# Chunked attention with the values as weights and a feature-major result, one pipeline step deeper

## What is computed

```python
scores = jnp.einsum("bcqhd,bckhd->bhcqk", qc, kb).astype(jnp.float32) * (dh ** -0.5)
scores = scores + rel_bias_band(rel_bias).astype(jnp.float32)[None, :, None]
...
probs = jax.nn.softmax(scores, axis=-1).astype(v.dtype)
out = jnp.einsum("bhcqk,bckhd->bcqhd", probs, vb)
...
mixed = jnp.concatenate([rms_norm(oa) * g_a, rms_norm(ob) * g_b], axis=-1) @ w_out
```

## Time and profile before

| what | value |
|---|---|
| median of 3 runs | 2630.72 us (2628.27 to 2630.9) |
| time of the profiled execution | 2636.18 us |
| span of its trace | 2634.4 us |
| granted TensorE clock, mean over the span | 0.971 |
| PE busy | 2549.1 us, 97% |
| DVE busy | 1528.3 us, 58% |
| ACT busy | 791.9 us, 30% |
| POOL busy | 211.1 us, 8% |
| share of PE in the chain that ended last | 89% |

### The profile page before, as it was taken

One profiled execution on the slowest core, in us unless ns is written; L12 is line 12 of the kernel. 1 busy time (PEld: TensorE's weight loads), 2 busy tenths in 40 slices (PEclk: granted clock), 3 DMA queues, 4 the chain that ended last, 5 costly groups with the idle time before them and its releaser, 6 DMA issues.

```text
span 2634.4 us, 33048 instructions
## 1 busy us (share of the span) xinstructions
PE 2549.1 (97%) x12768; PEld 2108.3 (80%) x12768; DVE 1528.3 (58%) x2329; ACT 791.9 (30%) x1337; POOL 211.1 (8%) x122
## 2 busy tenths in 40 slices
PE   7999999999999999998999999998999999999998
PEld 6777787888888888887788878877788888888886
DVE  6568265444444345746445478888566464646466
ACT  2245151110111011445434365554532121212122
POOL 6303300000000000000222200100000000000000
PEclk9887899999999999998999999998999999999999
DMA  3402603232323233113111000121012121212011
GB/s 122 37 9 65 81 18 108 85 90 78 100 80 96 78 100 116 37 48 113 36 35 35 25 17 25 33 97 37 20 56 65 32 64 32 64 32 68 28 56 72
DMA packets 201578, 157.08 MB, mean 60 GB/s; under 512 B 56184, under 2 KB 176512, under 8 KB 201472
## 3 DMA queue, kind: packets, MB, share of 16 engines
q1 hardware_dynamic: 183344, 124.94, 16.6%
q10 hardware_dynamic: 18128, 30.71, 4.4%
HBM read 147.23 MB, written 11.56 MB: 60 GB/s over the span
## 4 chain that ended last, share of the span: by engine, by line
PE 89%; DVE 5%; DMA 2%; ACT 2%; issue 1%; POOL 1%; SPq 1%; ACTq 0%; DVEq 0%; PEldq 0%; POOLq 0%
PE pd L837 26%; PE pd L839 25%; PE pd L838 25%; PE pt L1357 1%; PE pd L1412 1%; DMA raw<-in_w_out 1%; PE pt L837 1%; PE pd L1326 1%; PE pt L1427 1%; PE pt L1374 1%; PE pt L857 1%; PE pt L839 1%; PE pt L838 1%; PE pt L1079 1%; PE pt L1376 1%
## 5 line engine op out<-in xcount | busy, mean ns | idle before, releaser
L837 PE MATMUL pd<-actT_hi,st_hi 128*128 128x512 f32 x1872 | 750.5, 401 | 7.3 <-DVE st_lo L2240 3.8
L839 PE MATMUL pd<-actT_hi,st_lo 128*128 128x512 f32 x1872 | 735.5, 393 | 0.0
L838 PE MATMUL pd<-actT_lo,st_hi 128*128 128x512 f32 x1872 | 734.9, 393 | 0.0
L837 PEld LDWEIGHTS pd<-actT_hi,st_hi 128*128 128x128 f32 x1872 | 354.8, 190 | 80.2 <-ACT evac L1592 4.0
L839 PEld LDWEIGHTS pd<-actT_hi,st_lo 128*128 128x128 f32 x1872 | 354.7, 189 | 76.1
L838 PEld LDWEIGHTS pd<-actT_lo,st_hi 128*128 128x128 f32 x1872 | 355.4, 190 | 66.7
L837 PE MATMUL pd<-mv_hi,hid_hi 128*128 128x512 f32 x864 | 337.7, 391 | 3.3 <-DVE acc L2547 1.5
L838 PE MATMUL pd<-mv_lo,hid_hi 128*128 128x512 f32 x864 | 337.0, 390 | 0.0
L839 PE MATMUL pd<-mv_hi,hid_lo 128*128 128x512 f32 x864 | 336.8, 390 | 0.0
L1723 ACT ACTIVATE mv_hi<-raw 128x1024 fp32r<-128x1024 f32 x54 | 55.9, 1056 | 605.0 <-PE pd L839 477.9
L1592 ACT ACTIVATE evac<-pd 128x1024 f32<-128x1024 f32 x76 | 77.8, 1024 | 454.9 <-PE pd L839 454.9
(11 more groups left out here) (346 smaller groups left out, 3806.8 us busy)
## 6 DMA issues: line engine op xcount, KB each, us to landing
raw<-in_w_ff SPq DMA_DIRECT2D x64, 512.0 KB, 4.0
ada_raw<-in_w_ada ACTq DMA_DIRECT2D x64, 384.0 KB, 3.2
raw<-in_w_up SPq DMA_DIRECT2D x44, 512.0 KB, 3.8
raw<-in_w_in SPq DMA_DIRECT2D x30, 512.0 KB, 3.8
raw<-in_w_down SPq DMA_DIRECT2D x22, 512.0 KB, 3.3
acc<-in_x SPq DMA_DIRECT2D x16, 512.0 KB, 8.8
raw<-in_w_out SPq DMA_DIRECT2D x12, 512.0 KB, 3.3
raw<-in_w_ple_gate SPq DMA_DIRECT2D x8, 512.0 KB, 3.8
```

The source lines that it names most:

```text
L837: pe.matmul(out_ap, a_hi, b_hi, start=start, stop=False, skip_group_check=check)
L838: pe.matmul(out_ap, a_hi, b_lo, start=False, stop=False, skip_group_check=check)
L839: return pe.matmul(out_ap, a_lo, b_hi, start=False, stop=stop, skip_group_check=check)
```

## The change

The product with the values is turned round. Before, the turned probabilities were the weights (128 x 128) and the values the moving operand: `_hi` with 128 columns (`v_hi` and `v_lo` side by side) and `_lo` with 64. Now `v_hi` and `v_lo` (128 x 64) are the weights and the probabilities move with 128 columns, in three products per key tile, and the result stands feature-major in `pt[0:64]`. The division by the softmax sum can't be made on such a result, so DVE scales the probabilities before they are turned (`scale2`, `scaled`). ACT reads the banks out (`evac2`) where DVE did (`head_out`). `prob2` has three buffers for two. `turn2` is made for block z - 2 in PE's step z and `outputs2` for block z - 3; ACT's `parts2` and DVE's `low2` follow for block z - 3. The sums of squares of `oa` go to POOL and PE (`add_squares`, `square_sums`), and `turn_mixed` is gone.

```diff
             def turn2(z):
-                pe.wait_ge(p_ready, N1 + z + 1)
+                pe.wait_ge(scaled, N1 + z + 1)
...
-                o = pt[:, hh, (qt % 4) * P:(qt % 4 + 1) * P]
+                o = pt[0:64, hh, (qt % 4) * P:(qt % 4 + 1) * P]
...
-                    pe.matmul(o.rearrange("p (a b) -> p a b", b=64), pT2_hi[:, z % 2, j * P:(j + 1) * P],
-                              v[:, kt, :, hh, :], start=j == 0, stop=False, skip_group_check=True)
-                    last = pe.matmul(o[:, 0:64], pT2_lo[:, z % 2, j * P:(j + 1) * P], v[:, kt, 0, hh, :],
-                                     start=False, stop=j == n - 1, skip_group_check=True)
+                    pe.matmul(o, v_hi, p_hi, start=j == 0, stop=False, skip_group_check=True)
+                    pe.matmul(o, v_hi, p_lo, start=False, stop=False, skip_group_check=True)
+                    last = pe.matmul(o, v_lo, p_hi, start=False, stop=j == n - 1, skip_group_check=True)
...
-            for z in range(N2 + 2):
+            for z in range(N2 + 3):
                 if z % 2 and z + 1 < N2:
                     scores2(z + 1)
-                if 1 <= z < N2 + 1:
-                    turn2(z - 1)
+                if 2 <= z < N2 + 2:
+                    turn2(z - 2)
...
-                if z >= 2:
-                    outputs2(z - 2)
+                if z >= 3:
+                    outputs2(z - 3)
...
+            def evac2(g):
+                pair, half, hh = g // 4, g // 2 % 2, g % 2
+                act.wait_ge(pv_done, N1 + 16 * pair + 8 * half + 6 + hh + 1)
+                act.activation(out_features(0, pair, half)[64 * hh:64 * hh + 64, :], pt[0:64, hh, :], ACT.Copy)\
+                    .then_inc(o_half, 1)
+
+            for z in range(N2 + 4):
+                g = half2_ended(z - 4)
+                if g is not None:
+                    evac2(g)
+                if 3 <= z < N2 + 3:
+                    parts2(z - 3)
...
+            def scale2(z):
+                s, n = col2(z), step2(z)[3] * P
+                dve.wait_ge(p_ready, N1 + z + 1)
+                link(dve.reciprocal(rinv[:, s:s + 1], den[:, s:s + 1]))
+                dve.tensor_scalar(prob2[z % 3][:, 0:n], prob2[z % 3][:, 0:n], rinv[:, s:s + 1], None,
+                                  ALU.mult).then_inc(scaled, 1)
...
                 if z < N2:
                     top2(z)
                 if 2 <= z < N2 + 2:
-                    low2(z - 2)
+                    scale2(z - 2)
+                if 3 <= z < N2 + 3:
+                    low2(z - 3)
...
-                g = half2_ended(z - 3)
-                if g is not None:
-                    head_out(g)
...
             def beside3(s):
-                if 74 <= s < 78:
...
-                        turn_mixed(b, pd[:, 0, b % 2 * HB:(b % 2 + 1) * HB])
```

More of the change, by code:

```diff
@@ L204, in build @@
         NA = WA * P
-        prob2 = place("prob2", [P, 2, NA], F32, R_B)
+        prob2 = [place(f"prob2{n}", [P, NA], F32, at) for n, at in enumerate((R_B, R_B + NA * 4, R_M + 24 * KB))]
         pT2_hi = place("pT2_hi", [P, 2, NA], F32R, R_B + 5 * KB)
@@ L213, in build @@
         mix_gate = place("mix_gate", [P, D], F32, R_A + 28 * KB)
-        oa_junk = place("oa_junk", [P, HB], F32, R_A + 28 * KB)
+        sq_a = [place(f"sq_a{n}", [P, 2 * P], F32, R_A + (28 + n) * KB) for n in range(4)]
         sq_b = [place(f"sq_b{n}", [P, 2 * P], F32, R_S + (5 * n + 4) * KB) for n in range(4)]
@@ L1356, in turn2 @@
                 for j in range(step2(z)[3]):
-                    last = pe.transpose(ptT[:, j * P:(j + 1) * P], prob2[:, z % 2, j * P:(j + 1) * P], ident[:, :])
+                    last = pe.transpose(ptT[:, j * P:(j + 1) * P], prob2[z % 3][:, j * P:(j + 1) * P], ident[:, :])
                 last.then_inc(pt_done, 1)
@@ L1449, in outputs3 @@
                 last.then_inc(b_pv, 1)
-            def turn_mixed(b, bank):
-                half, src = b // 4, rows2[:, :, b % 4 * P:(b % 4 + 1) * P]
-                for r in range(4):
-                    last = pe.transpose(bank[:, r * P:(r + 1) * P], src[:, 4 * half + r, :], ident[:, :])
-                last.then_inc(tp_done, 1)
             def first_half_row(n):
@@ L1471, in beside3 @@
             def beside3(s):
-                if 74 <= s < 78:
-                    for b in range(2 * (s - 74), 2 * (s - 73)):
-                        if b < 2:
-                            pe.wait_ge(jb_lo, 4 * NJ1 + NL2 * 8)
-                        else:
-                            pe.wait_ge(tp_lo, TPJ["o2"] + b - 1)
-                        turn_mixed(b, pd[:, 0, b % 2 * HB:(b % 2 + 1) * HB])
-                elif 78 <= s < 94:
+                if 78 <= s < 94:
                     first_half_row(s - 78)
@@ L1865, in exps2 @@
                 act.wait_ge(nm_ready, N1 + z + 1)
-                act.activation(prob2[:, z % 2, 0:n], prob2[:, z % 2, 0:n], ACT.Exp, bias=nmx[:, s:s + 1],
+                act.activation(prob2[z % 3][:, 0:n], prob2[z % 3][:, 0:n], ACT.Exp, bias=nmx[:, s:s + 1],
                                accum_out=den[:, s:s + 1]).then_inc(p_ready, 1)
@@ L1874, in parts2 @@
                 act.activation(pT2_hi[:, z % 2, 0:n], ptT[:, 0:n], ACT.Copy).then_inc(pt_hi_s, 1)
-            for z in range(N2 + 2):
-                if 2 <= z < N2 + 2:
-                    parts2(z - 2)
+            def evac2(g):
[9 more added lines that the diff above has]
+                    parts2(z - 3)
                 if 1 <= z <= N2:
@@ L2399, in top2 @@
                 dve.wait_ge(s_done, N1 + (z // 2 + 1) * 2)
-                if z >= 2:
-                    dve.wait_ge(pt_done, N1 + z - 1)
+                if z >= 3:
+                    dve.wait_ge(pt_done, N1 + z - 2)
                 dve.memset(nmx[:, s:s + 1], 0.0)
-                link(dve.tensor_tensor_reduce(out=prob2[:, z % 2, 0:n], in0=x,
+                link(dve.tensor_tensor_reduce(out=prob2[z % 3][:, 0:n], in0=x,
                                               in1=bias2[pair % 2][:, hh, NA - n:NA], scale=1.0,
@@ L2413, in low2 @@
                                   ALU.subtract).then_inc(pt_lo_s, 1)
-            def head_out(g):
-                pair, half, hh = g // 4, g // 2 % 2, g % 2
-                dve.wait_ge(pv_done, N1 + 16 * pair + 8 * half + 6 + hh + 1)
-                c = slice(8 * hh + 4 * half, 8 * hh + 4 * half + 4)
-                head = 2 * pair + hh
-                o_out = rows2[:, 4 * half:4 * half + 4, 64 * head:64 * head + 64]
-                link(dve.reciprocal(rinv[:, c], den[:, c]))
-                o = pt[:, hh, :].rearrange("p (b n) -> p b n", n=P)
-                link(dve.tensor_copy(o_out, o[:, :, 0:64]))
-                link(dve.tensor_tensor(o_out, o_out, o[:, :, 64:P], ALU.add))
-                dve.sem_inc(o_half, 1)
-                last = dve.tensor_tensor(o_out, o_out, rinv[:, c].unsqueeze(2).to_broadcast([P, 4, 64]), ALU.mult)
-                if g % 4 == 3:
-                    last.then_inc(o_done, 1)
-                else:
-                    link(last)
+            def scale2(z):
[4 more added lines that the diff above has]
+                                  ALU.mult).then_inc(scaled, 1)
             mask_bias(0)
             mask_bias(1)
-            for z in range(N2 + 4):
+            for z in range(N2 + 3):
                 if z < N2:
@@ L2475, in inverse_roots, with mixed_lo @@
                     link(dve.tensor_tensor(out_, out_, t, ALU.mult))
-            def mixed_lo(b, bank=None):
+            def mixed_lo(b):
                 job, half, kt = TPJ["o2"] + b, b // 4 % 2, b // 8 * 4 + b % 4
-                if bank is None:
-                    bank = out_features(b // 8, b % 4, half)
+                bank = out_features(b // 8, b % 4, half)
                 c = slice(half * HB, (half + 1) * HB)
```

51 lines of the change are left out of this document (25 added, 26 removed).

## The result

The changed kernel takes 2676.1 us (median of 4 runs, 2667.2 to 2680.9), the kernel before 2630.8 us in the same comparison. The ratio is 1.0169, with a 95% interval from 1.0141 to 1.0198: 1.7% slower, clear of noise. The forecast was 2665 us, slower by 1.3%. The profiled execution took 2677.9 us.

The account below looks back on a forecast made before the run. PE bounds the kernel, so its stalls and instruction costs count. Terms -5.5 + 23.2 + 6.3 + 4.8 - 0.5 + 0.9 + 5 = +34.2 us: 2670 us profiled, median 2665 us, 1.3% slower; range 2643 to 2684 us.

Parts of the forecast that it names:

- The evacuations: Chunked stage: ACT's `evac2` ahead of the `_hi` copy stalls PE behind blocks 6, 7, 14, 15; +23.2 us, bounds 12 and 25.
- The values: Chunked stage: three shorter products per key tile save 0.04 us on 160 tiles; -5.5 us, bounds 4 and 9.6.
- The end of a pair: Steps 13 to 17 of a pair: scaling joins the loop between turns; +2.1 us three times, +6.3 us, bounds 1 and 9.
- the third `prob2` buffer spares `top2` its wait for the turn: Pair's end: reason given why the loop with scaling takes 2.7 us, about the 2.85 us it took before.
- the third buffer has no value by itself: Rival: `top2` waited for scores, not the buffer; said to cost nothing beyond the sum; no chance of its own given.
- POOL's hold: Scaling beside a POOL split lasts until it ends; charged at the pair's end; rival: everywhere, 9 us more, 2674 us, chance 0.10.
- The rival's place at the V unit: Rival of POOL holding the scaling everywhere: up to 1.2 us would reach PE at a pair's V unit; chance 0.10.
- The end of the stage: From the chunked stage's last blocks to the next stage's first product: 16.6 us against 11.8, +4.8 us.
- The clock: Half-speed stretches after PE stalls: three, +5 us, bounds 0 and 20; rival, every long stall, 15 us more, chance 0.14.
- The later stage: Stick-breaking stage: `turn_mixed` removal at nothing, ACT's squares -0.5 us, sums on PE +0.9 us.
- The inverse roots, at nothing under DVE's slack: Later stage: roots move from step 16 to 28 at no cost, up to 2 us without DVE's slack.
- the signs that the forecast named: Changed profile: `pT_lo` waits about 40 us, longest 2 to 2.5; 15 ACT evacuation waits of some 3 us; stage 257 + 29 us.

Follow-up runs that it names:

- Run 1: Changed kernel with ACT's `_hi` copy ahead of the evacuation: chunked stage 21.4 us shorter, whole 2654.4 us, 1.0075 of the kernel before.
- Run 8: Kernel before the change with `head_out` ahead of `low2` in DVE's step: chunked stage 48.9 us longer, whole 2691.1 us, 1.0218.
- Run 11: run 7 with the old form of the values (two products per key tile): chunked stage 5.3 us longer, whole 2639.0 us, 1.0013 of the kernel before.
- Run 2: Changed kernel with a fourth `prob2` buffer, `top2(z)` waiting for `turn2(z - 4)`: chunked stage 8.9 us shorter, whole 2667.8 us, 1.0135 of the kernel before.
- run 3: Changed kernel with the scaling on ACT, reciprocal and scaling a step earlier: chunked stage 17.8 us shorter, whole 2666.7 us, 1.0135 of the kernel before.
- Run 9: run 7 with 13 of the 14 inverse-root instructions moved behind the next four steps' copies: later stage 325.3 us, whole 0.9993 of the kernel before.
- run 4: Changed kernel with 32 unused transposes put back where `turn_mixed` was: later stage 327.4 us against 327.3, whole 2685.1 us, 1.0200 of the kernel before.
- run 10: Changed kernel, turn a step earlier, `_hi` copy ahead of the evacuation, scaling on ACT, inverse roots spread: whole 1.0038 of the kernel before.
- run 7: Changed kernel with `_hi` copy ahead of the evacuation, scaling on ACT and four `prob2` buffers: whole 2634.7 us, 0.9994 of the kernel before.
- run 5: Changed kernel with the old form of the values (two products per key tile): chunked stage 15.0 us longer, whole 2695.3 us, 1.0232 of the kernel before.

## Why the prediction was right in sign and near in size

*The evacuations, 23.2 us forecast.* In the changed kernel the gaps behind blocks 6, 7, 14 and 15 are 1.98, 1.14, 2.22 and 0.67 us, against 2.2, 1.2, 2.45 and 0.75. Three pairs have all four and the last pair the first two: 21.1 us. Run 1 took 21.4 us off. Run 8 shows the mechanism in the other kernel. The chain of single durations was right, each stall forecast some 0.1 to 0.2 us too long.

*The values, -5.5 us.* Run 11 puts them at 5.3 us with its stretch at the lower clock and at 4 us without, so the term was a little too large. The estimate from the Trainium skill's load time by columns ("TensorE: Matmul & The Clock Gate", LDWEIGHTS), 8.5 us, was too much.

*The end of a pair, +6.3 us forecast.* Here the forecast was short. From the last product of the projections in step 12 to the first in step 17 it is 16.5 us at the second and third pair's ends (13.3 before), 3.1 us more and 9.4 for three. The gaps grew by more, from 1.04 to 5.05 us, because the shorter products of the values in the loop turned into waiting, as the forecast said. The step that failed is "the third `prob2` buffer spares `top2` its wait for the turn", and with it the intervals of 2.7 us. `top2` still waits for a turn made in the step before, the turn's 0.74 us stays in the loop, and the intervals are 3.48, 2.94 and 2.94 us (2.7, 2.75 and 2.75 forecast) behind a first one of 4.16 (4.1 forecast). It is also why the rival "the third buffer has no value by itself" was wrongly called free. Run 2 shows it by giving `top2` the step of slack: the three later gaps vanish.

*POOL's hold.* The forecast charged it at the pair's end and covered it elsewhere. The rival's place at the V unit was real: block 4's turn waits 1.15 us in each of the four pairs, 4.6 us, behind a scaling of 2.63 us. The rival had up to 1.2 us there. At its other place, the squares, a scaling of 384 columns was held twice (0.91 us for 0.42), and no gap came of it. Off DVE and a step earlier (run 3) the scaling gave 17.8 us back, some of it clock, where my terms for the pairs' ends and the end of the stage make 11.1 us together. The Trainium skill's rule ("GPSIMD Engine Reference", Key points) names no exception, and in the changed kernel all three units of every pair show a scaling that lasts longer: 2.6 us at the V unit, 1.7 at the Q unit, 0.87 to 1.22 at the pair's end.

*The end of the stage, +4.8 us.* From the turn of block 59 (1550.58) to the next stage's first product (1568.32) it is 17.7 us against 11.8: 6.0 us, the difference to the forecast again mostly by the second interval, 3.48 for 2.7.

*The clock, +5 us.* Four stretches of 3.4 us at the lower level within the stage, where I had three, at most 6.8 us. They didn't follow each long stall. After the 2.22 us behind block 14 the clock fell in all three pairs that have it (the first row is the first pair's), and after the 2.50 us of the second pair's end it stayed:

```profile
1346.00:1349.30 3.30, 3.30 (x10) 2.58 (x10) 0.98 (x6) 0.00 (x0) 0.00 (x0) 0.54 0.00 0
1402.60:1405.00 2.40, 0.27 (x3) 0.30 (x4) 1.92 (x6) 0.92 (x2) 0.91 (x1) 1.00 0.06 19
1405.00:1408.40 3.40, 2.48 (x32) 2.29 (x31) 2.72 (x8) 2.12 (x4) 0.00 (x0) 1.00 0.50 145
```

Together: 21.1 + 9.4 + 4.6 + 6.0 - 4.0 + 6.8 = 43.9, where the stage shows 42.6; the clock's term is an upper bound.

*The later stage, +0.4 us forecast, +5.3 measured.* Two steps failed: the roots and sums, and the removal of `turn_mixed` at nothing. "The inverse roots, at nothing under DVE's slack": PE's sums took 1.84 us, not 0.94 (16 products, I had counted 8), and the 14 instructions of the roots then stood in front of the `_lo` copy (PE, DVE, changed kernel; the first and the last of them):

```profile
1644.98 1.84 PE L1398 MATMUL pt<-ones,sq_a 128*128 128x1 f32 x16
...
1648.68 0.17 DVE L2452 TENSOR_SCALAR rsq_v<-pt 128x8 f32<-128x8 f32 x1 [2.67 <-ACT wt_hi L1903]
...
1651.69 0.17 DVE L2458 TENSOR_TENSOR rsq_a<-rsq_a,rsq_t 128x8 f32<-128x8 f32 x1
1651.90 0.29 DVE L2446 TENSOR_TENSOR wt_lo<-pt,wt_hi 128x128 fp32r<-128x128 f32 x1
```

At that copy (number 25, in step 28) the stage is 5.0 us later than at the one before it, by the kernel before; 2.8 come back by copy 30, so 2.2 stay. Run 9 shows that the roots' own share of what stays is 0.5 us. The other 1.7 are near the length of PE's sums, but no run left the sums out. The second place is between copies 72 and 77, 2.9 us. There the `_lo` copies of `actT` now read two operands in SBUF, and two pairs of them beside POOL's squares took 1.71 and 1.61 us where 1.28 was usual. And the first products behind (`first_half_row`) ran at the lower clock, 0.43 us apart instead of 0.23, for 4.4 us. I had costed `turn_mixed` at nothing, and putting its transposes back took no time (run 4); I had not costed what its removal changed around it. How the 2.9 us divide between the held copies and the clock was not tried by itself.

So the two stages grew by 47.9 us where the forecast had 34.2: 13.7 us short. The later stage is 4.9 of it, block 4 4.6, the pairs' ends 3.1, the values 1.5 and the end of the stage 1.2; the evacuations were 2.1 us too high. The main term stands on its mechanism, but that the total lies within the range owes something to luck: these misses were of either sign, and in the profiled execution 5.8 us of the growth were hidden by chance, ahead of the chunked stage.

Of the signs that the forecast named, PE's waits for `pT_lo` (45.5 us for about 40) and the longest ones (2.5 us) came out. ACT waited 16 times at the evacuation, but 4.7 us each, not 3, and the stage lasted 301.6 us, not 286.

## What to carry to other kernels

An instruction that empties a result bank waits for the very end of another engine's step. Put it behind everything that this engine's next step needs, and look again at what that is whenever an instruction moves (run 10). Count a buffer's worth from its wait: which step makes the thing that is waited for, before and after; a buffer added together with a step of delay bought nothing here. And when an instruction goes into a loop that sets the pace, lay out all that stands between two turns of it in a row, from the trace, the waits of the neighbours too.

## What was not expected of the hardware

The scaling of 384 columns in SBUF, 0.42 us when alone, took 2.63 us when it began together with a POOL instruction of two inputs; 640 columns took 0.55 us alone and 0.87 to 2.00 beside such an instruction, by how long POOL still had to go. The same work on ACT was not held (0.82 us). A copy that DVE made out of PSUM beside POOL was not held either (`pT_lo`, 0.82 us beside `st_lo` in run 7), the copies of `actT` with both operands in SBUF were, by 0.3 to 0.4 us per pair. The Trainium skill ("GPSIMD Engine Reference", Key points) says that DVE instructions with two SBUF inputs, or in a 2-port mode, contend with POOL. The copies agree with it; that the scaling, which reads one tensor, ran in such a mode is shown by no run.

The clock fell in some stalls of 2 us and not in others of the same length, and it stayed low for 13.6 us (run 5) in a stretch whose instructions ran at the full clock in run 11. The unchanged part ahead of the chunked stage ended between 1255.5 us (run 4) and 1281.9 us (run 11), the clock of that stretch at 0.97 and 0.95:

```profile
0.00:1255.50 1255.50, 1210.98 (x5532) 993.06 (x5534) 669.48 (x1076) 330.13 (x521) 127.92 (x69) 0.97 0.30 77
```

```profile
0.00:1281.90 1281.90, 1231.16 (x5532) 1006.96 (x5534) 672.49 (x1076) 330.24 (x521) 127.95 (x69) 0.95 0.29 75
```

PE's busy time differs by 20.2 us with the same instructions, three quarters of the spread of 26.4. A change to the chunked stage of 3 us can be read there, and not in the whole.
